# Latent attention laid out anew: turned queries and keys in two banks of their own, scores last in a step, group tiles taken up a step later

## What is computed

```python
def mla_mixer(p, cos, sin, qa_norm, kva_norm, w_q_up, w_kv_up, q_gain, k_gain):
    q_lat, kv_lat, k_r = jnp.split(p, [MLA_Q_RANK, MLA_Q_RANK + MLA_KV_RANK], axis=-1)
    q = (rmsnorm_2(q_lat, qa_norm) @ w_q_up).reshape(b, s, N_MIX_HEADS, MLA_QK_DIM)
    kv = (rmsnorm_2(kv_lat, kva_norm) @ w_kv_up).reshape(b, s, N_MIX_HEADS, MLA_NOPE_DIM + MLA_V_DIM)
    q = jnp.concatenate([q[..., :MLA_NOPE_DIM], rope(q[..., MLA_NOPE_DIM:], cos, sin)], axis=-1)
    k_rope = jnp.broadcast_to(rope(k_r[:, :, None, :], cos, sin), (b, s, N_MIX_HEADS, MLA_ROPE_DIM))
    k = jnp.concatenate([kv[..., :MLA_NOPE_DIM], k_rope], axis=-1)
    v = kv[..., MLA_NOPE_DIM:]
    q = rmsnorm_2(q, q_gain).transpose(0, 2, 1, 3) * MLA_QK_DIM ** -0.5
    k = rmsnorm_2(k, k_gain).transpose(0, 2, 1, 3)
    return from_heads(causal_block_attention(q, k, v.transpose(0, 2, 1, 3)))
```

## Time and profile before

| | us |
|---|---|
| median of 3 runs | 1646.55 |
| lowest and highest | 1644.51, 1649.4 |
| the profiled execution, its own time | 1643.91 |
| span of the profile | 1642.2 |
| TensorE busy | 1565.1 (95%) |
| VectorE busy | 825.2 (50%) |
| ScalarE busy | 713.0 (43%) |
| GpSimd busy | 334.9 (20%) |

### The profile page before, as it was taken

One profiled execution on the slowest core, in us unless ns is written; L12 is line 12 of the kernel. 1 busy time (PEld: TensorE's weight loads), 2 busy tenths in 40 slices (PEclk: granted clock), 3 DMA queues, 4 the chain that ended last, 5 costly groups with the idle time before them and its releaser, 6 DMA issues. The chain is left out here.

```text
span 1642.2 us, 21202 instructions
## 1 busy us (share of the span) xinstructions
PE 1565.1 (95%) x8594; PEld 1312.0 (80%) x8594; DVE 825.2 (50%) x1341; ACT 713.0 (43%) x1309; POOL 334.9 (20%) x271
## 2 busy tenths in 40 slices
PE   7988998899999999999999999888899999999999
PEld 6777787799889788788888887666788788888887
DVE  5345444656444664755334442557764745334442
ACT  4435535356663544544224343455545534123431
POOL 0000133100340002244013431032102243014320
PEclk9999989899999999999999999989999999999999
DMA  6212112133231002233223331110002333223331
GB/s 223 78 33 83 52 52 65 40 141 114 79 104 38 27 1 77 90 103 109 96 78 102 99 119 56 45 55 16 24 1 88 92 91 125 85 84 93 110 106 52
DMA packets 37314, 128.49 MB, mean 78 GB/s; under 512 B 4176, under 2 KB 8928, under 8 KB 37216
## 3 DMA queue, kind: packets, MB, share of 16 engines
q1 hardware_dynamic: 37216, 127.13, 23.9%
HBM read 125.01 MB, written 2.10 MB: 77 GB/s over the span
## 5 line engine op out<-in xcount | busy, mean ns | idle before, releaser
L309 PE MATMUL bank<-hhi,whi 128*128 128x512 f32 (+1 forms) x1072 | 422.5, 394 | 4.3 <-DVE wlo L301 3.3
L311 PE MATMUL bank<-hhi,wlo 128*128 128x512 f32 (+1 forms) x1072 | 418.5, 390 | 0.0
L310 PE MATMUL bank<-hlo,whi 128*128 128x512 f32 (+1 forms) x1072 | 418.2, 390 | 0.0
L301 DVE TENSOR_TENSOR wlo<-wstage,whi 128x1024 fp32r<-128x1024 f32 (+3 forms) x206 | 273.7, 1332 | 145.5 <-ACT whi L290 145.1
L290 ACT CAST whi<-wstage 128x1024 fp32r<-128x1024 f32 (+3 forms) x206 | 228.8, 1116 | 136.7 <-PE bank L311 128.5
L309 PEld LDWEIGHTS bank<-hhi,whi 128*128 128x128 f32 (+1 forms) x1072 | 200.9, 187 | 50.1 <-DVE wlo L301 5.4
L2283 DVE SCALAR_TENSOR_TENSOR cr<-bank,vc,cr 128x511 f32<-128x511 f32 (+1 forms) x168 | 125.8, 749 | 218.4 <-ACT cr L2223 215.4
L311 PEld LDWEIGHTS bank<-hhi,wlo 128*128 128x128 f32 (+1 forms) x1072 | 200.6, 187 | 43.8
L310 PEld LDWEIGHTS bank<-hlo,whi 128*128 128x128 f32 (+1 forms) x1072 | 200.8, 187 | 42.6 <-issue 0.6
L2223 ACT ACTIVATE cr<-bank,vc 128x512 f32<-128x512 f32 x84 | 65.5, 780 | 249.8 <-PE bank L311 249.8
L2325 POOL TENSOR_TENSOR cr<-cr,cr 128x512 f32<-128x512 f32 x44 | 94.2, 2140 | 312.1 <-DVE cr L2283 277.4
(11 more groups left out here) (416 smaller groups left out, 2337.8 us busy)
## 6 DMA issues: line engine op xcount, KB each, us to landing
wstage<-in_wts SPq DMA_DIRECT2D x148, 512.0 KB, 3.5
wstage<-in_wts SPq DMA_DIRECT2D x32, 704.0 KB, 4.1
wstage<-in_wts SPq DMA_DIRECT2D x18, 768.0 KB, 4.3
xT<-in_x SPq DMA_DIRECT2D x4, 512.0 KB, 5.0
xt<-in_x SPq DMA_DIRECT2D x4, 512.0 KB, 5.6
out<-ob SPq DMA_DIRECT2D x8, 256.0 KB, 2.3
U<-in_rel_ext SPq DMA_DIRECT2D x6, 256.0 KB, 9.3
wstage<-in_wts SPq DMA_DIRECT2D x3, 384.0 KB, 3.0
```

What stands on the lines that cost most here:

```text
L301: e.tensor_tensor(K.wlo[i % 3][:, 0:w], K.stage[i % 3][:, 0:w], K.whi[i % 3][:, 0:w].bitcast(F32), SUB).then_inc(*K.dve.up(("wlo", i)))
L309: e.matmul(o, lh, rh, start=start, stop=False)
L310: e.matmul(o, lh, rl, start=False, stop=False)
L311: return e.matmul(o, ll, rh, start=False, stop=stop)
```

## The change

It does these things:

1. Norm before the latent mixer (norm2): the memory queries mm 0 and mm 1 are made first, of x times the gain, and divided by the norm afterwards. x's two halves are made during ffn0's last products. In all three norms the two first products are made one after the other, and a norm is two entries with a split between its halves.
2. "lat" takes its three latent products one by one, and the sums of squares stand in the middle of a following product. The load of the two gains moves into ffn0.
3. The queries are no longer scaled on GpSimd. Their factor multiplies the scores: as the scale of the exponential, and in one product more on VectorE, which multiplies the maximum of 128 rows by the factor, for each of the 48 latent items. The keys are scaled head by head.
4. A head's queries are turned four steps ahead of its first item and its keys three, one of them in a step, in banks 2 and 3 (ring RQ). The latent scores stand last in a step and go round two banks (0 and 1). Tiles of group0 and group1 go to banks 3 and 7 (RH), those of group2 to RQ.
5. Group tiles are copied out one entry later than they are made, and attention begins among the tiles of group0.
6. Splits: at most one per entry in both attentions, and at other entries.

The core of the diff (renamed helpers, the places of tiles in memory and the counterparts on other engines are left out):

```diff
-    if not SPLITS[g]:
+    if not SPLITS[g] or (made and SCHEDULE[g] in ("foxatt", "mlaatt")):
...
-            if t + 2 == t0:
-                return self.heads[h].prep
+            if self.heads[h].prep is not None and t - t0 in (-4, -3):
+                return self.heads[h].prep, "qk"[t - t0 + 4]
...
+        late = 0 <= t < N and A.R is not None and A.items[t][0] >= 4
+        if 0 <= t < N and A.scored(t) and not late:
             score(A.scored(t))
         if 3 <= t <= N + 2:
             turn(t - 3)
@@ -1104,6 +1085,17 @@
             for c in range(4):
                 z = e.transpose(b[:, c * P:(c + 1) * P], A.y[A.name, "y", p][:, c, :], K.ident[:])
...
+        if A.prep(t):
+            prep, which = A.prep(t)
+            name, src, nz = prep(which)
+            b = A.R.take(q, (name, "T"))
+            for r in nz:
+                q.wait_ge(*K.at(r))
+            for c in range(4):
+                z = e.transpose(b[0:96, c * P:(c + 1) * P], src(c), K.ident[:])
+            z.then_inc(*K.pe.up((name, "T")))
+        if late:
+            score(A.scored(t))
...
+        factor = 1.0
+        if A.heads[h].factor:
+            factor, made = A.heads[h].factor(i)
+            q.wait_ge(*K.at(made))
+        e.activation(p[:, 0:n], src[:, 0:n], ACT.Exp, bias=A.mx[:, h, i:i + 1], scale=factor,
+                     accum_out=A.rs[:, h, i:i + 1]).then_inc(
             *K.act.up((A.name, "P", t), frees=[(A.name, "s" if A.heads[h].bias else "S", t)]))
...
-            e.tensor_reduce(m, K.bank((A.name, "S", t))[:, 0:n], AX, MAX, negate=True).then_inc(*K.dve.up((A.name, "mx", t)))
+            factor = A.heads[h].factor
+            e.tensor_reduce(m, K.bank((A.name, "S", t))[:, 0:n], AX, MAX, negate=True).then_inc(
+                *K.dve.up((A.name, "mx0" if factor else "mx", t)))
+            if factor:
+                f, made = factor(i)
+                q.wait_ge(*K.at(made))
+                q.wait_ge(*K.at((A.name, "mx0", t)))
+                e.tensor_tensor(m, m, f, MUL).then_inc(*K.dve.up((A.name, "mx", t)))
...
+PAIRS = {1: [("up0", 0), ("up0", 22)], 2: [("mm", 0), ("mm", 1)], 3: [("up1", 0), ("up1", 22)]}
+GAINS = {1: ("norm_ffn", 0), 2: ("norm_mix", 8), 3: ("norm_ffn", 8)}
...
+    x = Parts(("u", s), *K.xu)
+    K.RA.go_on_at(0)
+    for n, key in enumerate(PAIRS[s]):
+        i, hi, lo = K.chunk(q, *key)
+        o = K.RA.take(q, key)
+        for k in range(8):
+            q.wait_ge(*K.at((x.gen, "hi", k)))
+            q.wait_ge(*K.at((x.gen, "lo", k)))
             z = mm3(e, o[:], hi[:, k, :], lo[:, k, :], x.hi[:, k, :], x.lo[:, k, :], k == 0, k == 7)
-            if k == 7:
-                z.then_inc(*K.pe.up(key, K.used(i)))
-        if k == 1:
-            pe_sum_whole(e, q, K, 1 + 2 * l, 7)
-    yield
-
-
-def first_pair(l):
-    return [(f"up{l}", 0), (f"up{l}", 22)]
-
-
-def divided(K, l, key):
-
-    return K.xd[:, first_pair(l).index(key), :]
+            if n == 0 and k == 1:
+                pe_sum_whole(e, q, K, s, 7)
+        z.then_inc(*K.pe.up(key, K.used(i)))
+        yield
...
     for k in range(8):
+        if k == 4:
+            yield
         q.wait_ge(*K.at((gen, "n", k)))
...
+                act_scaled(e, q, K, 2, m)
...
+    pe_fm(e, q, K, LAT[0], x, 8, T)
+    yield
+    pe_fm(e, q, K, LAT[1], x, 8, T)
+    for m in range(2):
+        o = K.RA.take(q, ("mms", m))
+        q.wait_ge(*K.at(("mmsq", m)))
+        e.matmul(o[:], K.blk[:], K.tmp["mmsq", m][:], start=True, stop=True).then_inc(
+            *K.pe.up(("mms", m), frees=[("mmsq", m)]))
+    yield
+    pe_fm(e, q, K, LAT[2], x, 8, T, mid=lambda: sums(("lsum", 0), (0, 1), K.STAT))
+    yield
+    K.RA.go_on_at(4)
+    pe_fm(e, q, K, ("kr", 0), x, 8, T, rows=32, mid=lambda: sums(("lsum", 1), (2,), K.RA))
+    yield
+    K.RA.go_on_at(6)
...
+EVEN = {"gq": (0, 1, 2, 3), "gkv": (4, 5, 6, 7), "qz": (1, 2, 3, 4), "kz": (5, 6, 7, 8), "k sq": (6, 7, 8, 9),
+        "q sq": (10, 11, 12, 13), "vz": (6, 7, 8, 9), "k sum": (7, 8, 9, 10), "q sum": (11, 12, 13, 14)}
+TWOS = {"gq": (0, 0, 2, 2), "gkv": (4, 4, 6, 6), "qz": (1, 1, 3, 3), "kz": (5, 5, 7, 7), "k sq": (6, 6, 8, 8),
+        "q sq": (10, 11, 12, 13), "vz": (5, 5, 7, 7), "k sum": (7, 7, 9, 9), "q sum": (11, 12, 13, 14)}
...
+    for h in range(4):
+        x = kt[:, :, h, :]
+        q.wait_ge(*K.at(("k", j, "r")))
+        q.wait_ge(*K.pool.last())
+        e.tensor_tensor(x, x, rk[:, h:16:4].unsqueeze(2).to_broadcast([P, 4, 96]), MUL).then_inc(
+            *K.pool.up(("k", j, "normed", h)))
...
-    out += ["out0"] + ["foxatt"] * 3 + ["out0"] * 7 + ["bar5", "norm1"] + ["ffn0"] * 63 + ["norm2", "bar6"]
-    out += ["lat"] * 5 + ["group0"] * 8
-    side = {}
-    for t0, n, name in ((-1, 9, "group0"), (7, 17, "group1")):
-        for s in range(n):
-            side.setdefault(t0 + s, []).append(name)
-    for s in range(17):
-        side.setdefault(27 + (s // 2 if s < 8 else s - 4), []).append("group2")
-    for t in range(-2, 69):
-        out += ["mlaatt"] + side.get(t, [])
-    out += ["out1"] + ["mlaatt"] * 3 + ["out1"] * 7 + ["bar7", "norm3"] + ["ffn1"] * 64
+    out += ["out0"] + ["foxatt"] * 3 + ["out0"] * 7 + ["bar5"] + ["norm1"] * 2 + ["ffn0"] * 63 + ["bar6"] + ["norm2"] * 2
+    out += ["lat"] * 3 + ["mlaatt"] * 2 + ["lat"] + ["mlaatt"] * 2
+    for n in range(4):
+        out += ["group0", "group0", "mlaatt"] + ["lat"] * (n == 0)
+    for n in range(8):
+        out += ["group0"] + ["group1"] + ["mlaatt"]
+    for t in range(14, 69):
+        out += ["group1"] * (t < 22) + ["group2"] * (t in (19, 20, 23, 24, 27, 28, 31, 32) or 33 <= t < 41) + ["mlaatt"]
+    out += ["out1"] + ["mlaatt"] * 3 + ["out1"] * 7 + ["bar7"] + ["norm3"] * 2 + ["ffn1"] * 64
...
-SPLITS = [not ("foxatt" in SCHEDULE[g:g + 2] and SCHEDULE[0:g].count("foxatt") not in (0, 20, 28, 36, 44)) for g in range(len(SCHEDULE))]
...
+        if "foxatt" in SCHEDULE[g:g + 2]:
+            out.append(SCHEDULE[0:g].count("foxatt") in (0, 22, 34, 44, 54))
+        elif name == "mlaatt" or name[0:5] == "group":
+            n = SCHEDULE[0:g].count("mlaatt")
+            out.append(n < 14 or name == "mlaatt" and n in (19, 27, 35, 43))
+        else:
+            out.append(True)
...
+    K.RQ, K.RH, K.RS3 = (Ring(K, b, K.in_bank) for b in (banks[2:4], [banks[3], banks[7]], banks[0:3]))
...
-            K.mlaatt = Attention("mla", mem_heads(K, 1, K.mqT1) + mla_heads(K), (K.RS, K.RT, K.RO), K.tmp, pt, None, sb("mla_mx", [P, 16, 4], scope=s2),
+            K.mlaatt = Attention("mla", mem_heads(K, 1, K.mqT1) + mla_heads(K), (K.RS2, K.RT, K.RO, K.RQ, K.RS3), K.tmp, pt, None, sb("mla_mx", [P, 16, 4], scope=s2),
                                  sb("mla_rs", [P, 16, 4], scope=s2),
-                                 lambda p, i: y1["mla", "y", p][:, i, :].rearrange("p (h n) -> p h n", h=2), "o1", y1)
+                                 lambda p, i: y1["mla", "y", p][:, i, :].rearrange("p (h n) -> p h n", h=2), "o1", y1,
+                                 out_bank=lambda p: 0 if p < 2 else (p + 1) % 2)
```

More of the change, by code:

```diff
@@ L1022, in turned_on_act @@
     def turned_on_act(self, t):
-        return self.st is not None or (self.given is not None and self.items[t][0] < 4)
+        return self.st is not None or (self.pta is not None and self.items[t][0] < 4)
     def post(self, t):
@@ L1136, in act_att @@
             act_evac(e, q, K, (A.name, "pt", t - 3), (A.name, "T", t - 3), o[:, 0:n], K.bank((A.name, "T", t - 3))[:, 0:n])
+        if A.prep(t):
+            prep, which = A.prep(t)
+            name, scale, r = prep(which + "h")
+            hi = K.mring[which].take(q, name)
+            for x in r:
+                q.wait_ge(*K.at(x))
+            q.wait_ge(*K.at((name, "T")))
+            e.activation(hi[0][:], K.bank((name, "T"))[0:96, :], ACT.Identity, scale=scale).then_inc(*K.act.up((name, "hi")))
         p = A.post(t)
@@ L1848, in dve_norm @@
     low(7)
-    if pair is not None:
-        for key in first_pair(pair):
-            q.wait_ge(*K.at(first_pair(pair)[1]))
-            e.tensor_tensor(divided(K, pair, key), K.bank(key)[:], K.hold["rb", s][:], MUL).then_inc(
-                *K.dve.up((key, "made"), frees=[key, ("rb", s)]))
+    for key in PAIRS[s]:
+        q.wait_ge(*K.at(PAIRS[s][1]))
+        e.tensor_tensor(divided(K, s, key), K.bank(key)[:], K.hold["rb", s][:], MUL).then_inc(
+            *K.dve.up((key, "made"), frees=[key, ("rb", s)]))
     yield
@@ L2485, in norm @@
             q.wait_ge(*K.at(("ln", j)))
-            e.copy(K.lhi[:, j, :], K.tmpd["ln", j][:]).then_inc(*K.act.up(("lhi", j)))
+            e.copy(K.lhi[:, j, :], K.tmpl["ln", j][:]).then_inc(*K.act.up(("lhi", j)))
+    for m in range(2):
+        t = K.tmp.take(q, ("mmsq", m))
+        q.wait_ge(*K.at((("mm", m), "made")))
+        e.activation(t[:], K.mqT1[:, m, :], ACT.Square).then_inc(*K.act.up(("mmsq", m)))
+    yield
     square(0)
+    yield
     square(1)
+    for m in range(2):
+        t = K.tmp.take(q, ("mmr", m))
```

(23 more changed lines are left out.)

384 lines of the change are left out of this document (149 added, 235 removed).

## The result

The changed kernel takes 1658.05 us (median of 4 runs, 1657.62 to 1660.48), that of before 1646.36 beside it. The ratio is 1.0071 (95% interval 1.0055 to 1.0087): slower, by about 12 us, where 1621 was forecast. The page's busy times, to be laid beside the earlier trace rows: TensorE 18 us more, VectorE 13 more.

The account below looks back on a forecast made before the run. TensorE, busy 95% of 1642.2 us, was taken as the bound. Terms 7 + 9.5 + 4.5 + 0 + 3.4 + 1 = 25.4 off 1643.9 gave 1618.5, with 2.6 for the median 1621; range 1607 to 1637.

Parts of the forecast that it names:

- foxatt, 3.4 won: In foxatt, single splits at four places replace two back to back: 3.4 of 5.4 us at stake won, bounds 0 and 5.4.
- Two single waits of 1 us are left: In foxatt, what TensorE would still wait at single splits, so 3.4 of the 5.4 us at stake are won.
- the clock term: In foxatt, the window's clock of 0.98 over 96 us costs 1.9 us, counted in the 5.4 at stake.
- Latent heads (4.5 won in the first part, 0 in the second): Group1 and group2 among latent heads: 57.5 for 62 us, bounds 0 and 10; late heads: 0, bounds +2 and -2.
- Start of attention, 9.5 won: From 1070.7 to 1119: 14.4 us to win, 5 left in eight bank waits of some 0.6; bounds 4 and 14.4.
- Norm2 and lat, 7 won: From 1024.4 to 1070.7: 5.2 us from 24 products under the norm, 1.8 from lat's idle; bounds 3 and 7.7.
- norm1 and norm3, 1 won: In these norms, two entries with a split between win 0.5 us each; bounds -1 and +2.6.
- The product: Maximum times factor on VectorE costs 0.2 us per latent item, bounds 0.15 and 0.4; 9.6 us for 48.
- the rival on that side: Late latent heads: copy, low half and split ahead of the maximum cost 0.65 us per latent step; 1652 us, chance 0.05.
- signs of being wrong: Pair's period over 0.5 us longer, waits over 2 us at banks 3 and 7, or norm2's latent product waiting each k-step.
- not over 85: Sign of being right: VectorE over 85% busy in the group1 and group2 stretch, TensorE's waits ending on its copies or maxima.

Follow-up runs that it names:

- placement runs: Changed kernel with foxatt's two splits back to back as before: 1639.67 us; kernel before with foxatt's splits single, at steps 22 and 34: 1660.72 us.
- the filled waits: Changed kernel with 16 useless turnings of the identity on TensorE ahead of each of foxatt's two waits: 1638.64 us.
- the execution that kept the clock at 1.00, the earlier copy: Changed kernel, low halves one entry later in foxatt and mlaatt, mlaatt's splits one step on, group0 and group1 values copied one entry earlier: 1621.74 us.
- the shift in mlaatt: Changed kernel with VectorE's low half of a split one entry behind ScalarE's high half in foxatt and mlaatt: 1626.81 us.
- the shift in the groups: Changed kernel with the low half one entry behind the high half in foxatt, mlaatt, lat and the groups: 1628.50 us.

## Why the prediction was wrong

Forecast were 25.4 us won, and the profiled executions differ by 14.3 lost (1642.2 to 1656.5): 39.7 us of error, of which foxatt has 20.7, the start of attention 11.0 and the latent heads 4.8.

- *foxatt, 3.4 won, bounds 0 and 5.4.* This is the step that failed. It read "Two single waits of 1 us are left". They are 2.23 and 2.36 us, since VectorE not only makes the low half but also stands for 1.24 and 1.34 us while ScalarE makes the high half (1.03). And the clock term was taken as something that a change can only give back, though the kernel before has 3.4 us at half clock behind a wait of 1.90. foxatt lost 17.3 us, 15.8 of them by the clock. Both placement runs and the filled waits show it.
- *Latent heads (4.5 won in the first part, 0 in the second).* Idle falls from 13.7 to 7.9 us, and the late pair from 14.92 to 13.04, where 0 was taken: the layout does more than forecast. But two splits bring waits of 2.15 and 3.04 us, and the clock of 0.86 in place of 0.98 takes it all back, some 13 us. Together that is 0.3 lost instead of 4.5 won. In the execution that kept the clock at 1.00 these heads take 94.7 us.
- *Start of attention, 9.5 won.* The clock loss went (0.88 to 1.00, 5 us), but idle grew from 7.4 to 12.6 us, where 5 were to be left: 1.5 us lost. TensorE waits 1.70, 0.85 and 2.48 us for banks 3 and 7. Here is the last of these waits, and the split that stood ahead of its copy on VectorE:

```profile
1099.60 0.45 PE L309 MATMUL bank<-whi,lhi 128*128 128x384 f32 x1 [2.48 <-DVE vt L2653]
...
1097.47 1.08 DVE L301 TENSOR_TENSOR wlo<-wstage,whi 128x768 fp32r<-128x768 f32 x1 [1.88 <-ACT whi L290]
```

  The term was mis-sized: a bank was taken to be held over one entry and its copy to cost 0.68 us. The values' copy comes two entries later, behind all that VectorE has there, a split and a maximum with their waits included. Of the 2.48 us the shift in mlaatt took 0.67 (1.81 are left), the shift in the groups no more (1.80), and the earlier copy the rest.
- *Norm2 and lat, 7 won.* 5.4 were won, and as told: the 72 products start at 1041.89 and the next at 1060.47, 18.6 us later, forecast 18.3, with three waits of 0.34 to 0.46 us in the latent product, for high halves. And lat keeps no idle time (22.90 of 22.90).
- *norm1 and norm3, 1 won.* Nearly nothing came: norm1 and ffn0 take 0.1 us less, out1 to the end 0.3 more. The wait of 1.30 gives way to two of 0.41 and 0.45 and one of 0.38 at the first product.
- *The product.* Sized rightly: a maximum of 256 columns to the next copy's start takes 0.52 us (1181.18 to 1181.70), 0.33 before, so 0.19. By the section "The DRAIN you can't avoid" of the Trainium skill's page "VectorE: DVE Perf Modes" it would be 0.15, the product's own time (an estimate from that rule). These rows show 0.04 more: the product starts 0.04 behind the maximum's end, takes 0.16 itself, and the copy starts 0.09 before its end, where in the kernel before it starts 0.08 before the maximum's.
- *The rivals and signs.* Slower it became, but not by the mechanism of the rival on that side: the late heads' steps are shorter, not longer. The split ahead of the maximum, which that rival spoke of, is right, at single steps instead of each, and it had no clock in its price. Of the signs of being wrong one came, a wait of over 2 us for banks 3 and 7 (2.48). VectorE is busy for 86.5 of the latent heads' 109.1 us, 79% and not over 85, and TensorE's longest waits there end on exponentials.

## What to carry to other kernels

A wait of TensorE costs its length and what the clock takes behind it, and the second can be four times the first (here 2.23 us, then 20.5 us at half clock, which lose up to 10.2): price both, and for every split or burst on a helper engine ask which step it falls in, not only how long it is. Where one engine needs what another is just making, put it one step later. Test two coupled edits (order in a step, banks) together before either is judged. Here the order alone made the kernel before 1.1% slower, taking it out of the changed kernel made that 1.0% slower, and the whole change with the low halves, the splits of mlaatt and the values' copies moved is 1.4% faster than before.
